# A mixture-of-experts transformer kernel: one dense gather of the tokens per layer, 8 KiB weight runs, paired score products

## The reference

```python
for i in range(2):
    mod = c_act @ ada_w[i] + ada_b[i]            # sh1, s1, g1, sh2, s2, g2
    h = modulate(rms_norm(x, norm1_g[i]), sh1, s1)
    y = diff_attention(h, hc, ...) if i == 0 else pool_mixer(h, ...)
    x = x + g1 * y
    h2 = modulate(rms_norm(x, norm2_g[i]), sh2, s2)
    x = x + g2 * moe(h2, router_w, router_b, w_gate[i], w_up[i], w_down[i])

# diff_attention, per head: p = softmax(q @ k.T * scale) for both maps
#   w = p[0] - lam * p[1];  o = w @ v
# moe, per expert e on its tokens xb:
#   (silu(xb @ w_gate[e]) * (xb @ w_up[e])) @ w_down[e], times the token's gate, summed per token
```

## Time and profile before

| | |
|---|---|
| median of 3 executions | 1437.2 us |
| the profiled execution, whole | 1435.71 us |
| its span, first to last instruction | 1433.9 us |
| TensorE busy, mean granted clock | 1311.4 us, 0.973 |
| VectorE, ScalarE, GpSimd busy | 344.6, 282.5, 31.8 us |
| read from HBM | 484.89 MB, 339 GB/s over the span |
| front part, experts 0, pooling, experts 1 | to about 338, 830, 907, 1434 us |

### The profile page before, as it was taken

How to read it: one execution, slowest core, us unless ns; L and a number is a source line. 1 busy time by engine, 2 the same in 40 slices (tenths; PEclk the granted TensorE clock), 3 DMA queues, 4 the chain that set the end, 5 groups by cost and what they waited for, 6 DMA issues and landing times.

```text
span 1433.9 us, 14452 instructions
## 1 busy us (share of the span) xinstructions
PE 1311.4 (91%) x5612; PEld 599.2 (42%) x5612; DVE 344.6 (24%) x716; ACT 282.5 (20%) x611; POOL 31.8 (2%) x23
## 2 busy tenths in 40 slices
PE   3999999885999999999999979499999999999996
PEld 2444445544443344343443356253443434434342
DVE  2556835424011110111101034411101110111102
ACT  3221126511111111111111111121111111111110
POOL 0122000000000000000000000000000000000000
PEclk9999999987999999999999999799999999999999
DMA  9956867473999999999999994459999999999994
GB/s 353 405 191 258 310 224 274 177 268 143 379 392 396 393 394 394 396 394 393 394 396 394 398 378 174 177 206 391 393 395 394 393 393 396 394 393 393 395 395 188
DMA packets 199584, 486.39 MB, mean 339 GB/s; under 512 B 7040, under 2 KB 8320, under 8 KB 199552
## 3 DMA queue, kind: packets, MB, share of 16 engines
q1 hardware_dynamic: 196928, 481.91, 89.3%
q10 hardware_dynamic: 2624, 4.05, 0.8%
HBM read 484.89 MB, written 1.05 MB: 339 GB/s over the span
## 4 chain that ended last, share of the span: by engine, by line
PE 74%; SPq 8%; DVE 6%; DMA 6%; ACT 3%; issue 2%; POOL 1%; POOLq 0%; DVEq 0%; ACTq 0%
PE PS L626 27%; PE PS L645 13%; PE PS L617 8%; PE PS L653 7%; SPq L278 6%; PE PS L475 5%; DMA ring<-in_moe_w_up 4%; PE PS L744 2%; PE PS L762 2%; PE PS L534 2%; DVE ring L1081 2%; PE PS L499 2%; SPq L283 2%; DMA ring<-in_ada_w 2%; PE PS L413 1%
## 5 line engine op out<-in xcount | busy, mean ns | idle before, releaser
L626 PE MATMUL PS<-ring,KT 128*64 128x512 f32 x1088 | 247.4, 598 | 10.6 <-ACT KT L916 8.3
L645 PE MATMUL PS<-ring,HT 128*64 128x512 f32 x1024 | 230.7, 593 | 0.9 <-ACT HT L935 0.9
L626 PE MATMUL PS<-ring,QT 128*64 128x512 f32 x960 | 218.7, 598 | 6.3 <-ACT QT L916 5.7
L1347 DVE COPY TMP<-PS 64x512 f32<-64x512 f32 x64 | 43.7, 683 | 562.8 <-PE PS L645 562.8
L617 PE MATMUL PS<-HT,KT 128*128 128x192 f32 x704 | 139.7, 345 | 11.4 <-DVE HT L1343 11.4
L617 PEld LDWEIGHTS PS<-HT,KT 128*128 128x128 f32 x704 | 119.2, 197 | 69.9 <-issue 58.2
L475 PE MATMUL PS<-ring,HT 128*128 128x512 f32 x320 | 141.4, 599 | 1.5 <-DVE HT L1098 1.5
L626 PEld LDWEIGHTS PS<-ring,KT 128*64 128x64 f32 x1088 | 74.3, 137 | 145.8 <-issue 132.8
L645 PEld LDWEIGHTS PS<-ring,HT 128*64 128x64 f32 x1024 | 73.4, 137 | 146.4 <-issue 145.0
L653 PE MATMUL PS<-TMP,HT 128*128 128x512 f32 x256 | 118.4, 606 | 1.6 <-DVE TMP L1347 1.6
L922 ACT COPY TMP<-PS 64x512 f32<-64x512 f32 x64 | 37.2, 581 | 412.3 <-PE PS L645 412.3
(11 more groups left out here) (196 smaller groups left out, 774.1 us busy)
## 6 DMA issues: line engine op xcount, KB each, us to landing
ring<-in_moe_w_gate SPq DMA_DIRECT2D x128, 1024.0 KB, 16.4
ring<-in_moe_w_up SPq DMA_DIRECT2D x128, 1024.0 KB, 14.8
ring<-in_moe_w_down SPq DMA_DIRECT2D x64, 2048.0 KB, 16.6
ring<-in_ada_w SPq DMA_DIRECT2D x24, 2048.0 KB, 13.6
ring<-in_attn_w_in SPq DMA_DIRECT2D x2, 4096.0 KB, 13.9
ring<-in_attn_w_in SPq DMA_DIRECT2D x2, 2048.0 KB, 21.3
ring<-in_attn_w_out SPq DMA_DIRECT2D x1, 4096.0 KB, 12.9
ring<-in_pool_w_in SPq DMA_DIRECT2D x1, 4096.0 KB, 24.4
```

The source lines that it names most:

```text
L626: ins = mm(PS[64 * f:64 * f + 64, 4, :], xs[:, k, SLOTS * j:SLOTS * j + SLOTS], gu_w[s][:, k, :, 256 * f:256 * f + 256], start=k == 0, sto ...
L645: ins = mm(PS[64 * f:64 * f + 64, 6, :], lhs, dn_w[s][:, c, 512 * f:512 * f + 512], start=c == 0, stop=c == 3)
L1347: return V.tensor_copy(y_sb[64 * second:64 * second + 64, 0:512], PS[0:64, 6, :])
```

## The change

1. Longer runs. The features are dealt to partitions so that a partition has neighbouring rows: feature 8p + k instead of 128k + p for gate, up and the router, and for down pairs of rows. A run of gate or up in HBM is then 4 rows x 512 floats = 8 KiB (before: one row, 2 KiB), of down 2 rows x 1024 floats = 8 KiB (before: 4 KiB).
2. What has to match this order: `xn` of the second norms is written in the new order by VectorE; `ada_fin` reads blocks 3, 4, 9 and 10 by columns with a step of 8; the bias and gain columns in `vec` are rearranged once at the start (`spread_l`, six small products, six multiplications with `diag`, six sums); `hidden` writes pairs (`h_pairs`).
3. Dense gather. The 512 token places are sorted by expert: `routing` now first computes the expert's start (`dstart`) and the place of each choice (`dpos`). `pick` makes the zero-one matrix for 256 places at a time, `gather(half, k)` multiplies, and ScalarE and VectorE (`spread`, `spread_v`) write `dense`. Half 0 comes before expert 0, half 1 after expert 0's gate and up. The former end of `routing` is now `positions` and comes later, with `choose` and `overflow_tiles`, which grew.
4. Windows. GpSimd copies each expert's 64 places out of `dense` into one of two tiles `xw` at an address that it reads from `first_slot`. Expert 0 reads `dense` itself.
5. `choose` works for two experts (128 places) at a time and makes only the matrix of gates, for `combine`.
6. Scores. `qT` is one tile without zeros; each score map is a product over its own 64 partitions. Two memsets of VectorE and a second copy on ScalarE are gone.
7. `rw` is loaded once per layer, by ScalarE.

```diff
-        gu_w = [s[:, 0:8192].rearrange("p (k a f) -> p k a f", k=KC, a=2) for s in slot]
+        gu_w = [s[:, 0:8192].rearrange("p (a k f) -> p a k f", k=KC, a=2) for s in slot]
+        dn_rows = [s[:, 8192:12288].rearrange("p (a b n) -> p a b n", a=2, b=2) for s in slot]
...
-                        sp.dma_start(gu_w[s][:, 4 * part:4 * part + 4, a, :],
-                                     w[L.l, e, 512 * part:512 * part + 512].rearrange("(k p) f -> p k f", p=P)
+                        sp.dma_start(gu_w[s][:, a, 4 * part:4 * part + 4, :],
+                                     w[L.l, e].rearrange("(p k) f -> p k f", p=P)[:, 4 * part:4 * part + 4, :]
...
-                sp.dma_start(dn_w[s], w_down[L.l, e].rearrange("(c p) n -> p c n", p=P)).then_inc(L.dn_in[s], 16)
+                sp.dma_start(dn_rows[s], w_down[L.l, e].rearrange("(a p b) n -> p a b n", a=2, b=2)).then_inc(L.dn_in[s], 16)
...
+                def window(e, b):
+                    slot0 = pool.value_load(first_slot[0:1, e:e + 1] if isinstance(e, int) else first_slot[0:1, bass.ds(e, 1)],
+                                            min_val=0, max_val=2 * SEQ)
+                    return nc.gpsimd.tensor_copy(xw[b], KQH[:, bass.ds(slot0 + xd0, 4096)].rearrange("p (k n) -> p k n", k=KC)[:, :, 0:SLOTS])
+                pool.wait_ge(L.slots_known, 1)
+                pool.wait_ge(L.xs_v, 8)
+                pool.wait_ge(L.xs_a, 8)
+                for e in (1, 2):
+                    window(e, e % 2).then_inc(L.xw_ready, 1)
+                with pool.Fori(0, (NE - 3) // 2) as it:
+                    for c in range(2):
+                        pool.wait_ge(L.gu_done, 2 * it + (2 + c))
+                        window(2 * it + (3 + c), (3 + c) % 2).then_inc(L.xw_ready, 1)
...
+                if i % 6 in SPREAD_PARTS:
+                    return v.rearrange("p (q k) -> p k q", k=KC)[:, k, :]
...
-                    ins = mm(bank(4 + 2 * (u % 2) + m), qT[m][:, h, P * qt:P * qt + P], kT[:, h, :], start=True, stop=True)
+                    half = slice(HD * m, HD * m + HD)
+                    ins = mm(bank(4 + 2 * (u % 2) + m), qT[half, h, P * qt:P * qt + P], kT[half, h, :], start=True, stop=True)
...
             def experts(L):
-                pe.wait_ge(L.s_ready, 1)
-                for r in range(4):
-                    if r >= 2:
-                        pe.wait_ge(L.xs_done, r - 1)
-                    gather(2 * r, GW, 7 - r % 2).then_inc(L.xg_done, 1)
-                pe.wait_ge(routed, L.l + 1)
+                pe.wait_ge(L.picked, 1)
+                for k in range(KC):
+                    if k >= 4:
+                        pe.wait_ge((L.xs_v, L.xs_a)[k % 2], (k - 4) // 2 + 1)
+                    gather(0, k).then_inc(L.xg_done, 1)
+                pe.wait_ge(L.gu_in[L.slot(0)], 32)
+                pe.wait_ge(L.xs_v, 4)
+                pe.wait_ge(L.xs_a, 4)
+                gate_up(L.slot(0), dense, range(4)).then_inc(L.gu_half, 1)
+                pe.wait_ge(L.gu2_in[L.slot(0)], 32)
+                gate_up(L.slot(0), dense, range(4, KC)).then_inc(L.gu_done, 1)
+                pe.wait_ge(L.picked, 2)
+                for k in range(KC):
+                    if k >= 2:
+                        pe.wait_ge((L.xs_v, L.xs_a)[k % 2], 4 + k // 2)
+                    gather(1, k).then_inc(L.xg_done, 1)
+                pe.wait_ge(L.sg_ready, 1)
+                pe.wait_ge(L.xs_a, 8)
                 accumulate_zero(True)
...
                     if not last:
                         pe.wait_ge(L.gu_in[L.slot(n)], (2 * it + n // 3) * 32 + 32)
-                        if n % GRP == 0:
-                            pe.wait_ge(L.xs_done, (2 * it + n // 3) * 4 + 4)
-                        gate_up(L.slot(n), xsT[n // GRP % 2], n % GRP, range(4)).then_inc(L.gu_half, 1)
+                        pe.wait_ge(L.xw_ready, e + 1)
+                        gate_up(L.slot(n), xw[n % 2], range(4)).then_inc(L.gu_half, 1)
...
             def experts(L):
-                choose(GW, sg[:, :, 0:GW], (L.parts, 1), (L.sg_done, 1), L.s_ready)
+                pick(dpos).then_inc(L.picked, 1)
+                link(V.tensor_scalar(dpos2, dpos, -float(HALF), None, ALU.add))
+                for k in range(0, KC, 2):
+                    spread_v(L, 0, k)
+                dve.wait_ge(L.xg_done, KC)
+                pick(dpos2).then_inc(L.picked, 1)
+                positions(L)
+                choose(PAIR, sg, L.chosen, 1, L.sg_ready)
                 overflow_tiles(L)
                 hidden(1)
+                for k in range(0, KC, 2):
+                    spread_v(L, 1, k)
```

More of the change, by code:

```diff
@@ L175, in program @@
+        t_sb = HT[:, 2560:3072]
+        silu_sb = HT[:, 3072:3328]
+        h_sb = HT[:, 3328:3584]
+        h_pairs = h_sb.rearrange("p (b q) -> p q b", b=2)
+        picked = HT[:, 3584:4096].rearrange("p (t n) -> p t n", t=NT)
+        part = [rope_g[:, 256 * a:256 * a + 256].rearrange("p (t n) -> p t n", t=NT) for a in range(2)]
+        part_d = rope_g[:, :].rearrange("p (t n) -> p t n", t=NT)
         y_sb = TMP[:, 0:1024]
-        route = sb("route", 16)
-        pos, gate, pcur = (route[:, 4 * i:4 * i + 4] for i in range(3))
@@ L178, in program @@
-        nt_tmp = sb("nt_tmp", 32)
+        route = sb("route", 20)
+        pos, gate, pcur, dpos, dpos2 = (route[:, 4 * i:4 * i + 4] for i in range(5))
+        first_slot = HT[:, 2304:2304 + NE + 8].bitcast(I32)
         mhalf = sb("mhalf", 16)
@@ L393, in _, with windows @@
                 inverse_root(8 + g, oms[:, 4 * g:4 * g + 4])
-            for n in range(6):
+            def windows(L):
+                def window(e, b):
[11 more added lines that the diff above has]
+                        window(2 * it + (3 + c), (3 + c) % 2).then_inc(L.xw_ready, 1)
+                pool.wait_ge(L.gu_done, NE - 2)
+                window(NE - 1, (NE - 1) % 2).then_inc(L.xw_ready, 1)
+                pool.wait_ge(routed, L.l + 1)
+                n_ov = pool.value_load(ov_info[0:1, OVER:OVER + 1], min_val=0, max_val=OVER)
+                with pool.If(n_ov > 0):
+                    pool.wait_ge(L.gu_done, NE)
+                    with pool.Fori(0, OVER) as i:
+                        with pool.If(i < n_ov):
+                            pool.wait_ge(L.dn_done, NE + i)
+                            window(i + NE, 0).then_inc(L.ov_xw, 1)
+            inverse_root(12, msn[:, 0:1])
+            inverse_root(13, msn[:, 1:2])
+            windows(layers[0])
+            for n in range(2, 6):
                 inverse_root(12 + n, msn[:, n % 2:n % 2 + 1])
+            windows(layers[1])
         @block.tensor
@@ L440, in _ @@
             pe.wait_ge(const_in, 16)
+            pe.wait_ge(spread_in, 1)
+            for i in range(6):
+                ins = mm(PS[:, 2 + i // 4, P * (i % 4):P * (i % 4) + P], spread_l[:, P * i:P * i + P], ident, start=True, stop=True)
+            ins.then_inc(spread_mm, 1)
             for k in range(KC):
@@ L937, in step @@
                     upper_outputs(c % 2).then_inc(L.y_a, 1)
-                    more = not isinstance(it, int) and j < 2
-                    if more:
-                        act.wait_ge(L.xg_done, (2 * it + c // 3) * 4 + 5 + 2 * j)
-                        spread(L, xsT[(c // 3 + 1) % 2], 4 * j, GW, 7).then_inc(L.xs_done, 1)
                     if not last:
@@ L972, in _ @@
             experts(layers[0])
+            act.wait_ge(layers[0].acc_done, 4)
+            load_router()
             norm_part(1, 1, 0)
```

314 lines of the change are left out of this document (174 added, 140 removed).

## The result

The kernel after takes 1393.35 us (median of 4 executions, 1388.89 to 1396.81), the kernel before 1436.99 beside it. The ratio is 0.969, 95% interval 0.9676 to 0.9712. The forecast was 1392 (1368 to 1419).

What follows compares the result with a forecast made beforehand. The weight stream was taken to set each layer's end: first slot's release, 29 experts of stream, fixed tail. Two layers' 38.2 us plus 6.5 in front gave 44.7 off 1435.7, as a median 1392 us (1368 to 1419).

Steps and rivals of the forecast that it cites:

- Run length: Expert weight stream: 8 KiB runs raise 394 GB/s to 420, 14.98 us an expert; bounds 408 and 430.
- TensorE in the steady state: Expert loop: without the gathers TensorE needs 13.2 us an expert, below 14.98, so this buys nothing itself.
- The start of a layer: Routing to expert 0: net 0.8 us earlier, then DMA idles 11.2 us; with the stream 19.1 a layer.
- GpSimd: Window copy for each expert: 1.5 us taken, ends 0.7 and 4; beyond 1.9 each us costs 2 in all.
- Rival (b): Expert loop: GpSimd's copies take longer than a period, kernel slower, about 1517 at 17 us a copy; chance 0.06.
- Scores and finishes: Front part: scores gain 7 us, dropped memsets 1.5, strided finishes cost 2; net 6.5.
- (a): Weight stream: rate stays at 408 GB/s, long runs cut or HBM gives no more, 1417 us; chance 0.25.
- (c): Weight stream: rate stays at 394 GB/s and the new stall remains, 1447 us; chance 0.06.
- (d): Expert loop: waiting TensorE's clock falls to 0.50 in places, four experts of 26 us eat the gain, about 1437; chance 0.05.
- a clock below 1.00 after expert 20: Late in a layer's experts: TensorE's granted clock falling there would show the forecast wrong; no size given.
- the wait for GpSimd: TensorE's chain: a wait there for GpSimd would show the forecast wrong; no size given.
- a second hole at expert 4 or 5: Weight stream: a second idle stretch there, after the one behind expert 0, would show the forecast wrong; no size given.

Runs made afterwards that it cites:

- the early down product: The kernel after with expert 0's down product moved ahead on TensorE, between the fourth and fifth product pair of the second gather: 1391.6 us.

## Why the prediction was right, point by point

**Run length.** Right, and the best tested term: forecast 420 GB/s at 8 KiB, measured 422; 14.91 us an expert for 14.98. Cut to 2 and to 4 KiB the price per run also gave 1445 and 1412 as measured. The rule by which HBM binds such loads (the Trainium skill, DMA: Bandwidth & Descriptors, Where 436 GB/s comes from) does not hold here: 426 GB/s were sustained over 300 us. The ceiling of 435 GB/s that the same section states was not reached over such a stretch.

**TensorE in the steady state.** Forecast 13.2 us an expert; the timeline gives 26.53 a pair, 13.27. That it "buys nothing itself" was the wrong step; the sentence behind it, that it "only keeps TensorE off the path", was worth about 40 us. The long runs alone gained 3.7 us, because TensorE at 15.07 was the pace for most of a layer. The sum came out right since the kernel before had both limits at the same point, where the lead of three slots was just used up. TensorE's busy share in mid layer is 92% (368.79 of 400) and not 88%.

**The start of a layer.** The ranks to pick part became 2.34 shorter (910.78 to 914.04 against 5.60 before), forecast 2.3. down(3) at s + 20.8, forecast 21.2; hole 11.0, forecast 11.2; stream's end s + 445.2, forecast 447.6. From A to Z and from Z to Z the layers gained 21.5 and 17.2 (the second with the slow pooling in it), in sum 38.7, forecast 38.2.

**GpSimd.** 0.62 us a copy for a chosen 1.5, and one wait of 0.20 us. Rival (b) needed 15 us a copy.

**Scores and finishes.** The step that was mis-sized. The pair takes 1.07 to 1.13 where I took 0.86, so 0.6 and not 0.86 is saved for each, and alone it is worth 3 to 5 us and not 7. The strided finishes cost 3.7 on TensorE for the two blocks in the projections (3.94 for 1.92, 3.73 for 2.02) and 4.3 at A, where I took 2 for all four. Without the memsets and with plain finishes the 0.79 wait is gone and the half projection takes 7.11 for 8.74, 2.4 together for a chosen 1.5; in the kernel after the strided finish took the second part back (8.57). Net 0 instead of 6.5.

**What made up for it.** By the profiled executions the forecast is 6 us too good: 44.7 for 38.9. By the medians it is right, 1392 for 1393.35: the profiled execution of before lies below its median and that of after above. That a front part which gave 0 for 6.5 leaves the total within 1.4 us is luck: no run here assigns the rest of the 43.6 us to a stage. The pooling stage's 3 us are part of this, and why the clock in it is 0.50 at 815 to 825 in some executions (0.88 in that of the early down product) stays open.

**The rivals.** (a) fell with 422 GB/s; its price, 1417, was about that of real 4 KiB runs (1412). (b) and (c) did not come. (d) came in a mild form: from expert 16 on TensorE waits for weights, up to 2.9 us at a time, and behind some of these waits the clock falls for one half gate-up. The timeline of after:

```profile
562.72 3.65 PE L678 MATMUL PS<-ring,KQH 128*64 128x512 f32 x16 [2.26 <-DMA ring<-in_moe_w_up]
...
592.55 6.53 PE L678 MATMUL PS<-ring,KQH 128*64 128x512 f32 x16 [2.85 <-DMA ring<-in_moe_w_up]
...
1291.10 5.35 PE L678 MATMUL PS<-ring,KQH 128*64 128x512 f32 x16 [1.90 <-DMA ring<-in_moe_w_up]
```

The slow one at 592.55 (granted clock 0.50 from 592.5 to 597) lost 2.9 us, which the next experts won back at 1.6 each while the stream went on at 422. It cost nothing. The one at 1291.10 is expert 26's, so a clock below 1.00 after expert 20 came, which the forecast had named as a sign of being wrong. It cost nothing either: expert 31 still waited 0.33 us for its weights, so TensorE had caught up and the stream set the end. Of the other signs, the wait for GpSimd came with 0.20 us, and a second hole at expert 4 or 5 did not come: the DMA share is 0.94 or more in every window of 3 us from 951 to 988.

## What to carry to other kernels

Where two engines are within a few per cent of each other and buffers give one a lead, neither row of the busy table is the bound: count how often the one waits for the other over the whole stage, and expect each half of a change to gain little until both are made. Price a DMA stream by its runs: two lengths already in the trace gave 8 KiB within 1%, three gave 16 KiB as closely, and the shorter side of the two counts. A layout that makes runs longer moves its cost to whoever reads in the new order; look at that reader, here a weight load with a step of 8, before booking the gain.

## What the hardware showed unexpectedly

A step of eight floats in TensorE's stationary operand doubled a group of 16 one-column products (1.92 to 3.94 us), but left a group of 8 transposes at 1.16 us; reading with the same step on VectorE cost half as much again (1.13 for 0.75 us, 128x1024). Two products of 64 rows each on different halves of the rows did not fully overlap: 1.07 to 1.13 us, where half of the former 1.72 would be 0.86. Longer transfers (16 KiB runs) lost more at the end of the stream, 7 us of tail in the profile, than their rate won, until the last four experts were cut again.
